# Seven reorderings in a two-layer diffusion-backbone kernel: first loads and products, copies on another engine, block order, one value product

## The reference

```python
for layer in range(2):
    mod = silu(c) @ w_mod[layer] + b_mod[layer]      # 6 vectors of 1024, for c and for c_ctx: shift, scale, gate, twice
    h = rmsnorm(x, g) * (1 + scale) + shift
    if layer % 2 == 0:                               # gMLP (u, v) beside a bidirectional RG-LRU (gate, xr)
        u, v, gate, xr = split(h @ w_in)
        y = concat(chunk_gmlp(u, v), rglru(xr, gate)) @ w_out
    else:                                            # windowed attention, 16 heads, 4 key heads, sink, rotary
        y = attention(h @ w_qkv) @ w_out
    x = x + gate * rmsnorm(y)
    h = rmsnorm(x, g2) * (1 + scale2) + shift2
    x = x + gate2 * rmsnorm(square(relu(h @ w_ffn_in)) @ w_ffn_out)   # width 4096
```

## Time and profile before

| | us |
|---|---|
| median of three runs | 1429.85 |
| the profiled execution | 1429.37 |
| its span, first to last instruction | 1427.3 |
| TensorE busy | 1373.6 |
| VectorE busy | 885.5 |
| GpSimd busy | 715.1 |
| ScalarE busy | 706.2 |
| mean granted TensorE clock | 0.988 |

### The profile page before, as it was taken

The page is one execution under the profiler, slowest core; times in us unless marked ns, Lnnn a source line. Parts: engine busy times, 40 slices in busy tenths (PEclk is TensorE's granted clock), DMA queues, the critical chain, the costliest instruction groups (busy, mean ns, idle before and its releaser), DMA issues.

```text
span 1427.3 us, 20872 instructions
## 1 busy us (share of the span) xinstructions
PE 1373.6 (96%) x7682; PEld 1162.0 (81%) x7682; DVE 885.5 (62%) x1543; ACT 706.2 (49%) x1431; POOL 715.1 (50%) x547
## 2 busy tenths in 40 slices
PE   5999999989999999999999989999899999999998
PEld 3876787868888888989767867788789899899896
DVE  4477864866655565565663578627855655656646
ACT  4375824744434444443552367637544534444443
POOL 1430413775445556555352567635855565555550
PEclk8999999999999999999999999999999999999999
DMA  9534272533454412212455200034323222231213
GB/s 350 161 95 142 69 257 68 192 118 119 136 209 157 148 59 90 89 62 87 153 185 185 89 2 1 1 118 172 108 90 104 74 91 87 72 106 59 89 60 148
DMA packets 98059, 164.32 MB, mean 115 GB/s; under 512 B 11100, under 2 KB 49704, under 8 KB 97960
## 3 DMA queue, kind: packets, MB, share of 16 engines
q1 hardware_dynamic: 86320, 157.23, 32.4%
q10 hardware_dynamic: 11640, 5.76, 1.6%
HBM read 154.82 MB, written 8.16 MB: 114 GB/s over the span
## 4 chain that ended last, share of the span: by engine, by line
PE 45%; DVE 2%; POOL 2%; issue 1%; ACT 0%; DVEq 0%; POOLq 0%; ACTq 0%
PE PS L2025 13%; PE PS L2026 13%; PE PS L2027 13%; PE PS L2367 2%; PE PS L2356 1%; PE PS L2335 1%; PE PS L2075 1%; PE PS L2336 1%; PE PS L2319 0%; PE PS L2312 0%; POOL WLU L1592 0%; POOL GG L1538 0%; PE PS L2115 0%; POOL HL L1561 0%; DVE HF L1786 0%
## 5 line engine op out<-in xcount | busy, mean ns | idle before, releaser
L1592 POOL TENSOR_TENSOR WLU<-RAW,WHU 128x512 fp32r<-128x512 f32 x340 | 457.5, 1371 | 376.3 <-ACT WHU L1227 376.2
L1227 ACT CAST WHU<-RAW 128x512 fp32r<-128x512 f32 x340 | 197.3, 618 | 236.9 <-PE PS L2027 121.7
L2025 PE MATMUL PS<-WHU,MXR 128*128 128x512 f32 x640 | 254.6, 398 | 11.9 <-issue 9.8
L2026 PE MATMUL PS<-WLU,MXR 128*128 128x512 f32 x640 | 252.0, 394 | 0.0
L2027 PE MATMUL PS<-WHU,MXR 128*128 128x512 f32 x640 | 251.6, 393 | 0.0
L1934 DVE TENSOR_TENSOR ACC<-ACC,PS 128x512 f32<-128x512 f32 x260 | 177.6, 684 | 94.8 <-PE PS L2027 93.7
L1587 POOL TENSOR_TENSOR WL<-RAW,WH 128x512 fp32r<-128x512 f32 x84 | 117.5, 1432 | 212.9 <-ACT WH L1218 195.4
L2025 PE MATMUL PS<-HH,WHU 128*128 128x320 f32 (+2 forms) x576 | 178.8, 310 | 3.9 <-POOL HL L1561 3.9
L2027 PE MATMUL PS<-HH,WLU 128*128 128x320 f32 (+2 forms) x576 | 178.6, 310 | 0.0
L2026 PE MATMUL PS<-HL,WHU 128*128 128x320 f32 (+2 forms) x576 | 178.5, 310 | 0.0
L2025 PEld LDWEIGHTS PS<-WHU,MXR 128*128 128x128 f32 x640 | 121.1, 189 | 47.2 <-issue 17.9
(11 more groups left out here) (274 smaller groups left out, 2637.3 us busy)
## 6 DMA issues: line engine op xcount, KB each, us to landing
RAW<-in_w_ffn_in SPq DMA_DIRECT2D x32, 1024.0 KB, 5.5
RAW<-in_w_ffn_out SPq DMA_DIRECT2D x32, 1024.0 KB, 5.0
RAW<-in_w_mod SPq DMA_DIRECT2D x18, 1024.0 KB, 5.8
GG<-in_w_mod SPq DMA_DIRECT2D x13, 1024.0 KB, 7.4
MX<-in_w_mod SPq DMA_DIRECT2D x11, 1024.0 KB, 5.2
RAW<-in_w_in_even SPq DMA_DIRECT2D x7, 1024.0 KB, 5.3
RAW<-in_w_qkv SPq DMA_DIRECT2D x6, 1024.0 KB, 7.5
xd<-X SPq DMA_DIRECT2D x10, 512.0 KB, 8.0
```

What stands on the lines that cost most here:

```text
L1227: nc.scalar.copy(unit_view(WHU, u), unit_raw(u["ld"], u["of"])).then_inc(u_hi, 1)
L1592: nc.gpsimd.tensor_tensor(unit_view(WLU, u), unit_raw(u["ld"], u["of"]), unit_view(WHU, u).bitcast(f32), ALU.subtract)\
L2025: MM(out, wh, xh, start=first, stop=False, skip_group_check=reopens)
L2026: MM(out, wh, xl, start=False, stop=False, skip_group_check=reopens)
```

## The change

1. At the kernel's begin scale's first two loads are issued ahead of w_in's first columns, and A0 of i=0 stands ahead of shift's second half.
2. Behind the first "u" group, the gate product (and the turn of the one before it) stands ahead of rg(1,1) and `vroot`.
3. In each FFN the groups of pair 0 from the fourth on are copied to ACC by ScalarE; VectorE keeps three.
4. GpSimd's remainder of T1 moves from `comb1` to behind the fifth group.
5. Pair 2's weight units come in the order A11, A12, A22, S2, S1, S3, S4, and S2 one event later.
6. The second part of the first direct product issues the products that need only HH first, then those of HL.
7. sums(3), PV(1) and rest(1) move from around(4) to ahead of the last qkv group.

```diff
-            step("g", uses_b=1, layer=layer, p=p, nh=q // TT, t=q % TT)
+            step("g", uses_b=1, layer=layer, p=p, nh=q // TT, t=q % TT, by_dve=q < 3)
...
             if q == 4:
                 flush()
+                step("t1_low", layer=layer)
...
-            order += [(p, name) for name in ("A11", "A12", "S2", "S1", "A22", "S4", "S3")]
+            order += [(p, name) for name in (("A11", "A12", "S2", "S1", "A22", "S4", "S3") if p > 2 else
+                                             ("A11", "A12", "A22", "S2", "S1", "S3", "S4"))]
...
                 if o == (2, "S2"):
-                    at = max(at, NS + 2)
+                    at = max(at, NS + 3)
...
     mod(0, 0, 0)
+    scale_ld = mod_load(0, 1, 0)
     ld = load("acols", src=("w_in",), col=1536)
...
-    mod(0, 1, 0)
+    mod(0, 1, 0, scale_ld)
...
+    step("A0", i=0, j=0)
     mod(0, 0, 1)
-    step("A0", i=0, j=0)
     mod(0, 1, 1)
...
-             ("u", 0): [(rg, 1, 1), (step, "vroot"), (mod, *fill[1])], ("u", 1): [(root, 1)], ("u", 2): [(rg, 2, 0), (mod, *fill[2])],
+             ("u", 0): [(mod, *fill[1]), (rg, 1, 1), (step, "vroot")], ("u", 1): [(root, 1)], ("u", 2): [(rg, 2, 0), (mod, *fill[2])],
...
-        if i:
+        if i and i != NKV:
             unit("sums", i - 1)
-        if 2 < i <= 2 + NKV:
+        if 2 < i <= 2 + NKV and i != NKV:
             unit("PV", i - 3, uses_m=1)
...
-        if 2 < i <= 2 + NKV:
+        if 2 < i <= 2 + NKV and i != NKV:
             unit("rest", i - 3)
...
+            if nb == 1 and t == NKV:
+                unit("sums", NKV - 1)
+                unit("PV", NKV - 3, uses_m=1)
+                unit("rest", NKV - 3)
             bgroup("qkv", nb, t, j)
...
+                elif k == "g" and not s["p"] and not s["by_dve"]:
+                    b = s["b"]
+                    act.wait_ge(t_add, 12 * s["layer"] + 12)
+                    upto(act, b_ready, b)
+                    nc.scalar.copy(ACC[:, s["t"], 512 * s["nh"]:512 * s["nh"] + 512], PS[:, 4 + b % 2, :]).then_inc(b_free[b % 2], 1)
...
-                elif k == "comb1":
+                elif k == "t1_low":
                     pool.wait_ge(t_hi, 10 * s["layer"] + 10)
                     nc.gpsimd.tensor_tensor(SLO["T1"], SRAW["T1"], SHI["T1"].bitcast(f32), ALU.subtract).then_inc(t_lo, 1)
...
+                    if (p, f, part) == (0, 0, 1):
+                        cols = DIRECT[1]
+                        for i in (0, 1):
+                            u = s["units"][i]
+                            pe.wait_ge(u_lo, u["number"] + 1)
+                            pe.wait_ge(f_hi[i], TT * layer + 5)
+                            for kt in range(4):
+                                for w in (WHU, WLU):
+                                    MM(out, unit_view(w, u)[:, kt, :], HH[:, 4 * i + kt, cols], start=w is WHU and (i, kt) == (0, 0), stop=False)
+                        for i in (0, 1):
+                            u = s["units"][i]
+                            pe.wait_ge(f_lo[i], TT * layer + 5)
+                            for kt in range(4):
+                                ins = MM(out, unit_view(WHU, u)[:, kt, :], HL[:, 4 * i + kt, cols], start=False, stop=(i, kt) == (1, 3))
```

More of the change, by code:

```diff
@@ L1927, in _ @@
                     V_.tensor_copy(QS[:, i % 2, :], m_bank(u)).then_inc(m_free[u % 2], 1)
-                elif k == "g":
+                elif k == "g" and not s["p"] and s["by_dve"]:
+                    b = s["b"]
+                    dve.wait_ge(t_add, 12 * s["layer"] + 12)
+                    upto(dve, b_ready, b)
+                    V_.tensor_copy(ACC[:, s["t"], 512 * s["nh"]:512 * s["nh"] + 512], PS[:, 4 + b % 2, :]).then_inc(b_free[b % 2], 1)
+                elif k == "g" and s["p"]:
                     b, acc = s["b"], ACC[:, s["t"], 512 * s["nh"]:512 * s["nh"] + 512]
                     upto(dve, b_ready, b)
[L1931 to L1936, removed]
+                    V_.tensor_tensor(acc, acc, PS[:, 4 + b % 2, :], ALU.add).then_inc(b_free[b % 2], 1)
                 elif k == "G2":
@@ L2178, in _ @@
                         pe.wait_ge(n_read, DIRECTS[layer, p, f, 0])
-                    if p == 0 and f == 0:
+                    out = direct_bank(s)
+                    if (p, f, part) == (0, 0, 1):
[12 more added lines that the diff above has]
+                                ins = MM(out, unit_view(WHU, u)[:, kt, :], HL[:, 4 * i + kt, cols], start=False, stop=(i, kt) == (1, 3))
+                        ins.then_inc(n_done, 1)
+                        continue
+                    if (p, f) == (0, 0):
                         for half in (0, 1):
-                            pe.wait_ge(f_lo[half], TT * layer + (2, 5)[part])
-                    out = direct_bank(s)
+                            pe.wait_ge(f_lo[half], TT * layer + 2)
                     for i in (0, 1):
```

## The result

| | before | after |
|---|---|---|
| median of 20 runs, us | 1429.54 | 1431.0 |
| ratio, 95% interval | | 1.0014 (1.0008 to 1.0021) |
| profiled execution, its span, us | 1429.37, 1427.3 | 1430.19, 1428.1 |
| mean granted TensorE clock | 0.988 | 0.991 |

The changed kernel is slower by 2.0 us (1.1 to 3.0), inside 0.2% but clear of zero; 1.6 us faster had been forecast. One of the 20 runs of the kernel before took 3490 us, which the median doesn't feel.

A forecast was written before the change was run, and what follows sets the result against it. TensorE, busy 1373.6 us (96% of the span), was taken as the bound. Terms 3.7 - 2.6 - 2.0 - 1.4 + 0.7 = -1.6 us gave 1428.2 us, with 1422.5 to 1432.5 for 8 in 10.

The forecast's parts named there:

- Kernel begin: Scale's loads first and A0 of i=0 ahead: second tile's half begins at 46.0 instead of 42.30, 3.7 us slower.
- The GpSimd wait: At the begin, VectorE's modulations of h and GpSimd's four remainders (4.94 us) wait for each other; without it 4 us lower.
- First "u" group: Gate product ahead of rg(1,1) fills TensorE's idle 2.56 us and avoids the stretch at 0.50: 2.6 us faster.
- FFN: At both FFN starts, tenth group stalls instead of the eighth: 2.0 us faster in the first layer, 1.4 in the second.
- The stall: Ahead of the FFN's tenth group, TensorE waits about 4.6 us in the second layer, where the eighth waited 3.99.
- a lower clock follows either: Behind the FFN's stall, old or new, TensorE runs slow; 0.3 us less lost to that in the first layer.
- rival 3: The tenth group's longer stall in each layer draws two full stretches at 0.50: 1433 us, slower; chance 0.22.
- Last qkv group: sums(3), PV(1) and rest(1) ahead delay the group and VectorE's rope; nothing of the 2.75 us wait won: 0.7 us slower.
- the likeliest case: The whole kernel's forecast itself, 1427.0 to 1430 with chance 0.32; its own range is 1426 to 1430.5 us.

The follow-up runs named there:

- w_no_begin: The changed kernel with the old begin (order of loads and A0 as before): 1427.13 us, ratio 0.9983 against the kernel before.
- w_order_back: The changed kernel with A0 of i=0 back behind shift's second half, scale's loads still first: 1427.34 us, ratio 0.9987 against the kernel before.
- w_loads_back: The changed kernel with w_in's first load ahead of scale's again, A0 of i=0 still ahead: 1431.94 us, ratio 1.0016 against the kernel before.
- u_only_u: The kernel before with only the first "u" group's part (gate product ahead of rg(1,1)): 1428.44 us, ratio 0.9989.
- u_only_product: The kernel before with only the new order of the first direct product (HH products first): 1426.34 us, ratio 0.9976.
- u_only_ffn: The kernel before with all four FFN parts alone (copies, T1's remainder, block order, product order): 1427.45 us, ratio 0.9983.

## Why the prediction was wrong

The parts alone sum to what the whole does: begin +4.4 (changed kernel less w_no_begin), "u" group -1.6, FFN -2.4, last group +1.4, together +1.8, for 2.0 measured. Against the forecast's terms:

- **Kernel begin, +3.7.** Right in size (3.3 in the traces, 4.4 timed with some 1.6 around it), and right that A0 of i=0 waits for h and that nothing hides shift's second half behind it. The end of A0 at 39.2, forecast at 39.3, is luck: h's last remainder ended at 37.1, 1.3 before the forecast, and the products not 0.9 but 2.1 behind it, because TensorE ran at 0.50 until 38.05. From there the chain ran as worked out (45.63 for 46.0). The GpSimd wait is there, and eats the 3.7 us that the swapped load gives. But the step put the cost on the swap's overlap and A0's place together; w_order_back and w_loads_back show that the swap is neutral, and that A0's place ahead of shift's products costs the whole, within what the timing tells.
- **First "u" group, -2.6.** Right at the place (-2.9; the load landed at 118.6 as its wait of 1.4 us says, no lower clock). What the step left out is the chain of VectorE and the queues, which don't gain: by the gates' read, 85 us later, 1.5 to 2.4 us are given back (in the changed kernel's and u_only_u's trace). Timed, -1.6 (0.3 to 2.7), so the forecast's size is not ruled out by the time alone.
- **FFN, -3.4, timed -2.4: the step that failed.** The stall itself was forecast right: ahead of the tenth group, 4.6 us in both layers, through the gate operations, S4's subtraction, its cast and the eighth group's copy. Right too was that the product's saved 3.9 us are taken up by the next stall: at the eighth group's start u_only_product has none of them left. What failed is the sentence "a lower clock follows either", that is, that TensorE loses the same to the slow stretch in every order. With the product's new order alone the stretch moves ahead of the eighth group, under VectorE's pace, and that wins 3.4 us where nothing was priced. With the copies, the block order and T1's place on top of it the stretch lies behind the tenth group's start again, in TensorE's own work: in u_only_ffn, whose tenth groups start where the forecast put them (309.8 and 1035.5, once the 0.6 and 1.6 us are put back by which this trace is early ahead of the FFNs), TensorE is busy at 0.50 for 5.5 and 4.5 us behind them. So these three parts, to which the text gave 2.0 and 1.4, come out at +1.0, give or take 2. The step also stopped at the tenth group: in both layers of u_only_ffn some 0.55 us more are lost 25 us later, where the next group products start (335.11 and 1059.27) after a wait of 0.40 that u_only_product hasn't. The two full stretches of the changed kernel are rival 3, which had a chance of 0.22 and a price of 1433, 2 us too high; they are worth 1.2 us of the miss in the traces, and since as long a stretch follows the 4.0 us waits of before in half of the cases (below), not shown to be more. Which of the three parts loses, and whether T1's move to the fifth group alone does, was not tried; T1 moved on to behind the ninth wins 8.7.
- **Last qkv group, +0.7.** Right in sign and waits (0.77 ahead, 2.9 behind), timed +1.4 (0.1 to 2.7), so only the size may be off.

So the sign fell on four terms, each 0.7 to 1.0 us too low, 3.4 of the 3.6 us between forecast and result. Each of these differences alone lies within what the timing can tell; together they don't. Inside the FFN's term the miss is clear of noise: 3.4 us for a part that was priced at nothing, and nothing like 3.4 for the three that were to win it. The causes given for the "u" group and the FFN, the second chain that had not moved and the place of the slow stretch, are read from the traces, and no kernel changed either alone. The range of 1422.5 to 1432.5 held the result, by terms that were all too low; that of the likeliest case, 1426 to 1430.5, didn't.

## What to carry to other kernels

Where two engines lock each other, look for the longest operation of the one and the shortest of the other: here moving one GpSimd operation of 3.2 us by four groups was worth 8.7 us, against at most 3.4 won by any part of the change alone. A product put ahead of another to fill a wait wins only if the chain that ended the wait is not needed again soon; follow that chain, and the order in which its transfers are issued, to the next place where TensorE waits for it. And a wait of a few microseconds is priced with the slow stretch behind it: in these traces the stretch cost little where another engine set the pace anyway, and half of its busy time where TensorE did. The best kernel here takes the change without its begin and with both T1's remainder and the gate operations behind the ninth group: 1417.88 us, 0.8% below the kernel before and 1.0% below the changed one.

## What the runs showed of the hardware

- The length of the slow stretch behind one and the same wait differs between executions. Of 14 waits of 4.55 us in seven traces, nine were followed by 6.8 us at the lower clock and five by 3.4; of six waits of 4.0 us, three and three. Three waits of 1.9 us in the first layer were followed by 3.4 us each, three in the second by none, and two of 1.2 us by none. So where one kernel's trace has a stretch and another's has none, the kernels need not be the cause.
- The same 6.8 us at 0.50 cost 2.6 us behind the eighth group of the kernel before and, as far as two traces set side by side show, next to nothing in u_only_product (299.4 to 306.2), where VectorE and GpSimd set the pace: it starts the eighth group 0.3 us later against its place ahead of the FFN.
- A VectorE operation on 8 columns took 0.17 us with GpSimd at rest, and 2.66, 1.19 and 1.04 us beside GpSimd's, each ending 0.02 us after one of these.
- A read of 4 x 256 KB took 9.0 us to land in two traces where it was issued just ahead of two loads of 1 MB, and 9.4, 9.8 and 10.1 in three where it was issued just behind them.
